# Other byte offsets for the stationary operands of a two-product MLP

## The chip, the core and the metric

The kernel runs on one NeuronCore of a Trainium2 chip. The metric is the device time of one execution in microseconds (us). The trace is one execution, taken by the hardware profiler. Its engines are TensorE (PE, with the loads of its stationary operand as PEld), VectorE (DVE), ScalarE (ACT), GpSimd (POOL) and SyncE (SP, which here issues DMAs).

## What is computed

A decoder layer on x of 2048 tokens by 1024 channels in float32. Its first half (input projection, mLSTM heads, causal convolutions, output projection) isn't touched. Its second half is the MLP:

```python
h2 = rms_norm(x, pre_mlp_norm_w[layer])
a = jax.nn.relu(jnp.einsum("bsd,df->bsf", h2, w_ff1[layer]))
m_out = jnp.einsum("bsf,fd->bsd", a * a, w_ff2[layer])
x = x + rms_norm(m_out, post_mlp_norm_w[layer])
```

with w_ff1 of 1024 x 4096 and w_ff2 of 4096 x 1024.

## The kernel before

It runs three phases one after the other: `phase_a` (input projection and convolutions), `phase_b` (mLSTM and output projection) and `phase_c` (the MLP). Each float32 product is made of three products of rounded parts: an operand is split by ScalarE into a high part (`_hi`) and by VectorE into the rest (`_lo`), and TensorE adds hi by hi, hi by lo and lo by hi in one PSUM bank. A matmul instruction is a load of the stationary operand (128 columns, 512 bytes of each partition) and a stream of the moving operand.

Both MLP products use a scheme with 7 sub-products in place of 8 (`OPS`, `OPS_2`). In the first product, `product(pe, op, g)` runs 12 matmuls of 512 columns (4 channel tiles, 3 pairs; L1861) for each of 7 sub-products and 32 groups: 2688 matmuls. Their stationary operand is a slice of 512 bytes of the weight tile `w1_hi[op]` (8 of the 12) or `w1_lo[op]` (4 of the 12), 14 tiles of 2 KB in all; the moving operand is a row of 2 KB of `x_hi` or `x_lo`. In the second product, `step(n)` runs 48 matmuls of 512 columns (L2079) for each of 56 steps, again 2688. Their stationary operand is a slice of 512 bytes of the middle activations `hid_hi` or `hid_lo`, which lie in a ring of 3 slots; the moving operand is a row of `w2_hi` or `w2_lo`. SyncE loads a slot of `hid_raw` two steps ahead (`load_hid`); ScalarE and VectorE split it in two halves each (`high_hid` L1952, `low_hid` L1957). VectorE reads the sums out of PSUM into the accumulators `acc`.

The order of every queue is written out by hand. Nothing chooses the addresses: in `phase_c`, `at(name, kb, ...)` places a tile at byte `4224 + 1024 * kb` of each partition. 4224 is 128 modulo 1024, so a tile at a whole `kb` has remainder 128, and one at a half `kb` has 640. Of the tiles that TensorE reads in phase C all have remainder 128, except buffer 0 of `x` and of `w2` (640, as moving operand). A slice of 512 bytes begins at 128 or 640.

In phases A and B the operands of the large matmuls (L404, L413, L423, L1332) begin at 128 or 640 too. One group doesn't: `("v", 0)` (L396) moves a row of 264 columns of the combined tile `vg_hi` or `vg_lo`. That tile begins at remainder 896, and each of its 8 rows (1056 bytes) lies 32 further modulo 1024: 896, 928, 960, 992, 0, 32, 64, 96. Its stationary operand (tokens) lies at 128 or 640.

Of the kernel before, what the change touches and what calls it, by code (L numbers as in the profile page):

```python
# [9 lines left out]
F32R = mybir.dt.float32r  # L10

P = 128
S = 2048
D = 1024
# [1631 lines left out]
OPS = ["P1", "P2", "P3", "P6", "P7", "P4", "P5"]  # L1646
# [60 lines left out]
def phase_c(nc, sem, psum, dram, late):  # L1707
# [6 lines left out]
    def at(name, kb, shape, dt=F32):  # L1714
        return nc.alloc_sbuf_tensor_at(name, [P, *shape], dt, offset=SB0 + int(1024 * kb))
# [2 lines left out]
    x_hi = [at(f"x_hi{i}", kb, (4, TB), F32R) for i, kb in enumerate(x_at)]  # L1718
    x_lo = [at(f"x_lo{i}", kb + 8, (4, TB), F32R) for i, kb in enumerate(x_at)]
    x_raw = [at(f"x_raw{i}", kb + 8, (4, TB)) for i, kb in enumerate(x_at)]  # L1720
    w1_hi = {op: at(f"w1_hi_{op}", 69 + 2 * i, (4, P), F32R) for i, op in enumerate(OPS)}
    w1_lo = {op: at(f"w1_lo_{op}", 83 + 2 * i, (4, P), F32R) for i, op in enumerate(OPS)}
    w1_raw = at("w1_raw", 187.5, (8, 4, P))
    c_1, c_x, c_7, c_21 = (at(n, 97 + 2 * i, (TB,)) for i, n in enumerate(("c_1", "c_x", "c_7", "c_21")))
    c_11 = at("c_11", 66, (TB,))
# [4 lines left out]
    w2_lo = [at(f"w2_lo{q}", kb + 8, (PIECE, TB), F32R) for q, kb in enumerate(w2_at)]  # L1730
    w2_raw = at("w2_raw", 170, (NFP, TB))
    grain = at("w2_grain", 161.5, (2, GRAIN, TB))
    hid_at = [121, 48, 105]
    hid_hi = [at(f"hid_hi{i}", kb, (NFP, P), F32R) for i, kb in enumerate(hid_at)]
    hid_lo = [at(f"hid_lo{i}", kb + 8, (NFP, P), F32R) for i, kb in enumerate(hid_at)]
    hid_raw = [at(f"hid_raw{i}", kb + 8, (NFP, P)) for i, kb in enumerate(hid_at)]
    acc = [at(f"acc{t}", 64 + 4 * t if t < 10 else 97.5 + 4 * t, (D,)) for t in range(S // P)]
    wpost = at("wpost_c", 170, (D,))
    junk = at("junk_c", 174, (D,))
    xn = at("xn_c", 178, (XN_RING, D))  # L1740
# [678 lines left out]
def build(nc, arrays, out):  # L2419
    scratch = {name: nc.dram_tensor("scratch_" + name, shape, dt).ap() for name, (shape, dt) in SCRATCH.items()}  # L2420
    dram = {**arrays, **scratch, "out": out.rearrange("a (n p) d -> (a n) p d", p=P)}
    with ExitStack() as ctx:  # L2422
# [3 lines left out]

        late = {}
        c = phase_c(nc, sem, psum, dram, late)
        b = phase_b(nc, sem, psum, dram, big, keep, c["prefetch"], late)
        a = phase_a(nc, sem, psum, dram, big, keep, b["tail"])  # L2430
# [42 lines left out]
```

## Time and profile before

| | us |
|---|---|
| median of 3 runs | 2109.27 |
| lowest and highest | 2109.08, 2110.45 |
| span of the profiled execution | 2109.4 |

The page of the profile gives the busy time of each engine, the clock that TensorE was granted, the chain of work that ended last, and the costliest groups of instructions. "x896 | 350.5, 391" means 896 instructions, 350.5 us in which at least one ran, 391 ns from start to end of one. Matmuls overlap in the pipeline, so what one costs is the distance from its start to the next one's start (here called the pitch), and not its 391 ns. The timeline gives the starts.

### The profile page before, as it was taken

To read this page: it belongs to the slowest core of one execution; us is meant where nothing else is said; L and a number is where in the kernel's file an instruction comes from. 1 tells how busy PE (TensorE), PEld (TensorE's weight loads), DVE (VectorE), ACT (ScalarE), POOL (GpSimd) and SP (SyncE) were. 2 spreads that over 40 slices of the span, in tenths; PEclk is the share of its full clock that TensorE was granted. 3 is DMA by queue.
4 is the path that set the end of the run, shared out by engine and by line. 5 is a ranking of instruction groups with operands and counts; after the bars stand their busy time and mean duration, and the time that the engine had idled before them with its cause. 6 is when DMAs were issued, how large, how long until landed. Compare 5 with 4: busy or idle time off the path is not lost. (4 is left out here: it accounts for less than half of the span.)

```text
span 2109.4 us, 26456 instructions
## 1 busy us (share of the span) xinstructions
PE 2065.3 (98%) x9843; PEld 1719.6 (82%) x9843; DVE 1441.5 (68%) x1979; ACT 913.2 (43%) x1545; POOL 414.6 (20%) x252
## 2 busy tenths in 40 slices
PE   7999999999999999899999999999999999999998
PEld 4897878878788888688888788888788888888887
DVE  5797999989567777876667866666663536534286
ACT  5633334343445444655445644554432313313163
POOL 0000000000001322333322322332262144400012
PEclk9999999999999999999999999999999999999999
DMA  5031212113656865854455655445766455443376
GB/s 201 11 101 51 70 40 77 54 30 107 195 165 205 264 225 167 269 175 136 153 164 179 235 165 157 138 145 172 254 227 249 163 206 187 167 167 137 140 250 219
DMA packets 253118, 338.53 MB, mean 160 GB/s; under 512 B 11584, under 2 KB 193600, under 8 KB 239168
## 3 DMA queue, kind: packets, MB, share of 16 engines
q1 hardware_dynamic: 220352, 315.80, 44.9%
q10 hardware_dynamic: 32384, 20.98, 3.1%
q8 instruction: 80, 1.31, 0.2%
q14 instruction: 46, 0.38, 0.1%
q0 software_dynamic: 256, 0.07, 0.0%
HBM read 225.58 MB, written 111.21 MB: 160 GB/s over the span
## 5 line engine op out<-in xcount | busy, mean ns | idle before, releaser
L1861 PE MATMUL psum<-x_hi,w_hi_P 128*128 128x512 f32 x896 | 350.5, 391 | 12.3 <-DVE x_lo L1805 6.2
L2079 PE MATMUL psum<-w_hi,hid_hi 128*128 128x512 f32 x896 | 349.3, 390 | 2.0 <-DVE hid_lo L1957 2.0
L1861 PE MATMUL psum<-x_lo,w_hi_P 128*128 128x512 f32 x896 | 349.6, 390 | 0.0
L1861 PE MATMUL psum<-x_hi,w_lo_P 128*128 128x512 f32 x896 | 349.5, 390 | 0.0
L2079 PE MATMUL psum<-w_lo,hid_hi 128*128 128x512 f32 x896 | 349.3, 390 | 0.0
L2079 PE MATMUL psum<-w_hi,hid_lo 128*128 128x512 f32 x896 | 349.1, 390 | 0.0
L1957 DVE TENSOR_TENSOR hid_lo<-hid_raw,hid_hi 128x1024 fp32r<-128x1024 f32 x112 | 176.7, 1615 | 207.4 <-ACT hid_hi L1952 207.3
L1774 POOL TENSOR_TENSOR w_raw<-w_raw 128x512 f32<-128x512 f32 x128 | 181.5, 1439 | 410.7 <-DVE w_lo_P L1787 388.5
L1952 ACT ACTIVATE hid_hi<-hid_raw 128x1024 fp32r<-128x1024 f32 x112 | 113.0, 1051 | 342.6 <-DMA hid_raw<-scratch_hid 342.6
L1787 DVE TENSOR_TENSOR w_lo_P<-w_raw,w_hi_P 128x512 fp32r<-128x512 f32 x224 | 184.6, 836 | 107.2 <-ACT w_hi_P L1783 104.2
L1783 ACT ACTIVATE w_hi_P<-w_raw 128x512 fp32r<-128x512 f32 x224 | 136.8, 627 | 255.7 <-PE psum L1861 249.3
L1861 PEld LDWEIGHTS psum<-x_hi,w_hi_P 128*128 128x128 f32 x896 | 168.9, 188 | 51.1 <-issue 14.4
L2079 PEld LDWEIGHTS psum<-w_hi,hid_hi 128*128 128x128 f32 x896 | 168.5, 188 | 37.4 <-issue 2.4
L1861 PEld LDWEIGHTS psum<-x_hi,w_lo_P 128*128 128x128 f32 x896 | 168.8, 188 | 35.0
L1861 PEld LDWEIGHTS psum<-x_lo,w_hi_P 128*128 128x128 f32 x896 | 168.8, 188 | 34.9
L2079 PEld LDWEIGHTS psum<-w_hi,hid_lo 128*128 128x128 f32 x896 | 168.6, 188 | 35.1
L2079 PEld LDWEIGHTS psum<-w_lo,hid_hi 128*128 128x128 f32 x896 | 168.5, 188 | 35.1
L1913 POOL TENSOR_TENSOR w_raw<-w_raw,w_grain 128x1024 f32<-128x1024 f32 x48 | 139.2, 2915 | 225.0 <-DMA w_grain<-in_w 225.0
L750 DVE SCALAR_TENSOR_TENSOR c_buf<-u_buf,par_a,c_buf 128x1024 f32<-128x1024 f32 x120 | 153.3, 1278 | 0.0
L750 DVE SCALAR_TENSOR_TENSOR c_odd<-u_buf,par_a,c_odd 128x1024 f32<-128x1024 f32 x112 | 143.1, 1277 | 4.2 <-ACT c_odd L556 4.2
L2204 DVE TENSOR_TENSOR c<-c,psum 128x512 f32<-128x512 f32 x96 | 65.5, 682 | 70.5 <-PE psum L1861 70.5
L423 PE MATMUL psum<-big_hi,w_hi 128*128 128x512 f32 x256 | 104.1, 407 | 4.0 <-DVE big_lo L704 3.7
(280 smaller groups left out, 3762.0 us busy)
## 6 DMA issues: line engine op xcount, KB each, us to landing
scratch_hid<-stage SPq DMA_DIRECT2D x224, 256.0 KB, 3.6
hid_raw<-scratch_hid SPq DMA_DIRECT2D x56, 1024.0 KB, 4.9
w_raw<-in_w SPq DMA_DIRECT2D x52, 1024.0 KB, 5.0
w_grain<-in_w SPq DMA_DIRECT2D x48, 512.0 KB, 5.0
x_raw<-scratch_h2s SPq DMA_DIRECT2D x14, 1024.0 KB, 8.5
w_raw<-in_w_in SPq DMA_DIRECT2D x22, 512.0 KB, 3.6
scratch_h2s<-h2s SPq DMA_DIRECT2D x8, 1280.0 KB, 9.2
scratch_qk<-qout ACTq DMA_DIRECT2D x16, 512.0 KB, 3.0
```

What stands on the lines that cost most here:

```text
L423: mm = nc.tensor.matmul(out, a, b, start=kt == 0 and i == 0, stop=kt == KT - 1 and i == 2)
L750: nc.vector.scalar_tensor_tensor(out=out, in0=u_buf[:, u % U_RING, k:k + HALF], scalar=par[:, CONV_W + g * CW + k:CONV_W + g * CW + k + 1] ...
L1774: nc.gpsimd.tensor_tensor(raw_1(op), raw_1(a), raw_1(b), ALU.subtract).then_inc(sem["w1_t"], 1)
L1783: nc.scalar.activation(w1_hi[op][:], raw_1(op), ACT.Copy).then_inc(sem["w1_hi"], 1)
L1787: nc.vector.tensor_tensor(w1_lo[op][:], raw_1(op), w1_hi[op][:].bitcast(F32), ALU.subtract).then_inc(sem["w1_lo"], 1)
L1861: mm = nc.tensor.matmul(psum[:, bank_1(op, g), :], l, r, start=kt == 0 and i == 0, stop=kt == 3 and i == 2)
L1913: nc.gpsimd.tensor_tensor(part, part, grain[:, n % 2], alu).then_inc(sem["w2_t"], 1)
L1952: nc.scalar.activation(hid_hi[n % HID_RING][:, half_fps(h)], hid_raw[n % HID_RING][:, half_fps(h)], ACT.Copy).then_inc(sem["hid_hi"], 1)
L1957: nc.vector.tensor_tensor(hid_lo[n % HID_RING][:, half_fps(h)], hid_raw[n % HID_RING][:, half_fps(h)], hid_hi[n % HID_RING][:, half_fps(h) ...
L2079: mm = nc.tensor.matmul(psum[:, bank, :], l, r, start=f == 0 and k == 0, stop=f == NFP - 1 and k == 2)
L2204: nc.vector.tensor_tensor(out[:], a[:], ps1(op, g), ALU.add).then_inc(sem["gather"], 1)
```

## The change

Only addresses change. The 14 weight tiles of the first product move down by 128 bytes or less, to the remainders 0, 0, 0, 32, 32, 32, 64 (`w1_hi`) and 64, 64, 96, 96, 96, 128, 128 (`w1_lo`), in the order P1, P2, P3, P6, P7, P4, P5. The 3 slots of the middle activations (high, low and raw alike) move up to the remainders 224, 192 and 160. The first ten accumulators move up by 96 bytes, out of the way of slot 1. The moving operands stay. On each of the five queues the built program has the same instructions in the same order with the same waits as before.

```diff
-    w1_hi = {op: at(f"w1_hi_{op}", 69 + 2 * i, (4, P), F32R) for i, op in enumerate(OPS)}
-    w1_lo = {op: at(f"w1_lo_{op}", 83 + 2 * i, (4, P), F32R) for i, op in enumerate(OPS)}
+    w1_hi = {op: at(f"w1_hi_{op}", 68.875 + 2 * i + i // 3 / 32, (4, P), F32R) for i, op in enumerate(OPS)}
+    w1_lo = {op: at(f"w1_lo_{op}", 82.875 + 2 * i + (7 + i) // 3 / 32, (4, P), F32R) for i, op in enumerate(OPS)}
...
-    hid_at = [121, 48, 105]
+    hid_at = [121 + 3 / 32, 48 + 1 / 16, 105 + 1 / 32]
...
-    acc = [at(f"acc{t}", 64 + 4 * t if t < 10 else 97.5 + 4 * t, (D,)) for t in range(S // P)]
+    acc = [at(f"acc{t}", 64 + 3 / 32 + 4 * t if t < 10 else 97.5 + 4 * t, (D,)) for t in range(S // P)]
```

## Rows read from the trace of the kernel before

**Rows 1.** The page: busy time of TensorE, granted clock, chain that ended last

```profile
PE 2065.3 (98%) x9843; PEld 1719.6 (82%) x9843; DVE 1441.5 (68%) x1979; ACT 913.2 (43%) x1545; POOL 414.6 (20%) x252
...
PEclk9999999999999999999999999999999999999999
...
PE 28%; DVE 1%; DMA 0%; SPq 0%; issue 0%; ACT 0%; DVEq 0%
```

**Rows 2.** Sums of stretches: us, busy (instructions) by engine, clock, DMA share, GB/s

```profile
core 0: us, PE busy (x) PEld busy (x) DVE busy (x) ACT busy (x) POOL busy (x), PEclk, DMA share, GB/s
...
900.00:1180.00 280.00, 280.00 (x1237) 231.93 (x1236) 191.67 (x271) 142.32 (x239) 82.96 (x60) 1.00 0.54 171
...
1520.00:2080.00 560.00, 560.00 (x2473) 463.68 (x2472) 287.65 (x289) 181.83 (x264) 149.34 (x52) 1.00 0.54 194
```

**Rows 3.** Timeline of TensorE, first product: start us, us, instruction; half clock until 895.98

```profile
892.14 0.63 PE L1861 MATMUL psum<-x_hi,w_lo_P 128*128 128x512 f32 x1
...
895.98 0.59 PE L1861 MATMUL psum<-x_hi,w_lo_P 128*128 128x512 f32 x1
896.41 0.40 PE L1861 MATMUL psum<-x_hi,w_hi_P 128*128 128x512 f32 x1
...
897.11 0.40 PE L1861 MATMUL psum<-x_hi,w_hi_P 128*128 128x512 f32 x1
897.35 0.39 PE L1861 MATMUL psum<-x_lo,w_hi_P 128*128 128x512 f32 x1
897.57 0.39 PE L1861 MATMUL psum<-x_hi,w_lo_P 128*128 128x512 f32 x1
...
898.73 0.39 PE L1861 MATMUL psum<-x_lo,w_hi_P 128*128 128x512 f32 x1
...
900.77 0.39 PE L1861 MATMUL psum<-x_lo,w_hi_P 128*128 128x512 f32 x1
```

**Rows 4.** Timeline of TensorE, output projection (L1332) after smaller matmuls

```profile
621.18 0.39 PE L1332 MATMUL psum<-big_lo,y_hi 128*128 128x512 f32 x1
...
622.79 0.39 PE L1332 MATMUL psum<-big_hi,y_lo 128*128 128x512 f32 x1
...
625.06 0.39 PE L1332 MATMUL psum<-big_hi,y_hi 128*128 128x512 f32 x1
```

**Rows 5.** Timeline of TensorE, 256-column matmuls (L413) after a small matmul

```profile
365.05 0.28 PE L413 MATMUL psum<-w_lo,big_hi 128*128 128x256 f32 x1
...
365.88 0.28 PE L413 MATMUL psum<-w_hi,big_lo 128*128 128x256 f32 x1
366.00 0.28 PE L413 MATMUL psum<-w_hi,big_hi 128*128 128x256 f32 x1
...
369.00 0.28 PE L413 MATMUL psum<-w_lo,big_hi 128*128 128x256 f32 x1
```

**Rows 6.** Timeline of TensorE, 264-column matmuls with changing remainders (L396)

```profile
129.80 0.28 PE L396 MATMUL psum<-w_lo,big_hi 128*128 128x264 f32 x1
...
134.39 0.28 PE L396 MATMUL psum<-w_hi,big_hi 128*128 128x264 f32 x1
```

**Rows 7.** Tile hid_raw: engine op xcount: duration ns min/median/max, first and last start

```profile
L1952 ACT ACTIVATE hid_hi<-hid_raw x112: 1040/1046/1064, 1476.9 to 2077.9; 128x1024 fp32r<-128x1024 f32 x112
L1957 DVE TENSOR_TENSOR hid_lo<-hid_raw,hid_hi x112: 1209/1225/3423, 1478.0 to 2079.7; 128x1024 fp32r<-128x1024 f32 x112
...
DMA to landing us min/median/max: 4.6/4.9/7.4
```

**Rows 8.** The page, costliest groups: the same VectorE operation on two tiles

```profile
L750 DVE SCALAR_TENSOR_TENSOR c_buf<-u_buf,par_a,c_buf 128x1024 f32<-128x1024 f32 x120 | 153.3, 1278 | 0.0
L750 DVE SCALAR_TENSOR_TENSOR c_odd<-u_buf,par_a,c_odd 128x1024 f32<-128x1024 f32 x112 | 143.1, 1277 | 4.2 <-ACT c_odd L556 4.2
```

## The prediction, made before the changed kernel was run

> **What bounds the kernel now.** I read the page first. TensorE is busy for 2065.3 of 2109.4 us, at 0.9 or more of the full clock in every slice, and the chain that ended last is made of it [rows 1]. Then the sums of two stretches, one inside each MLP product. There TensorE is busy for all of 280.00 and 560.00 us, while VectorE works 191.67 of 280 and 287.65 of 560 [rows 2]. So in phase C nothing but the pitch of the matmuls counts, and it can be read from the counts: 1237 records touch 280 us. A record is 0.39 us long, so about 1.7 of them only reach into the stretch: 280 / 1235.3 = 226.7 ns. The other stretch gives 560 / 2471.3 = 226.6 ns.
>
> [...]
>
> [...]
> [...]
> [...]
> - Behind an interruption they need some matmuls to settle. In the first product, 10 pitches from 896.41 to 898.73 have a mean of 232 ns (single ones lie apart: 897.11 to 897.35 is about 240, the next about 220), and then the 9 up to 900.77 have 226.7 [rows 3]. In the output projection, 7 pitches from 621.18 to 622.79 have 230 ns, and the next 10 have 227 [rows 4]. With 256 columns it is the other way: 7 pitches from 365.05 to 365.88 have 118.6 ns, and the settled ones 120.0 [rows 5].
>
> [...] The unsettled one is 3.3 to 5.3 ns longer at 512 columns, and 1.4 ns shorter at 256. All settled rows have both operands at the remainder 128 or 640.
>
> The one group that doesn't have them there is the 264-column one: 38 pitches from 129.80 to 134.39, 120.8 ns each [rows 6]. [...]
>
> **The change part by part.**
> - Weight tiles of the first product. The seven high tiles leave 128; of the low tiles five do. A group of 7 sub-products has 84 matmuls: 7 x 8 read a high tile and 5 x 4 a moved low tile, 76 in all; with 32 groups 2432. TensorE is the bound here, so each nanosecond on them is on the path.
> - Slots of the middle activations. All 2688 matmuls of the second product read a moved stationary operand. Together 5120.
> - What the new distance does to the pitch isn't in the trace for 512 columns. Bounds: above, the longest unsettled mean, 232 ns (+5.3 ns, 5120 x 5.3 = +27 us); one pitch of the same stretch is about 240 ns [rows 3], and if a fixed distance held the pair at 236, halfway between that and the mean, it would be +9.3 ns, +48 us. Below, the 264-column row, -2.5 ns (5120 x 2.5 = -13 us). Between them: the settled pitch stays, 0. I take the mean of the two unsettled 512-column rows, 231 ns, +4.3 ns, since these are the rows with the same length of stream, and the 264-column row is nearest to them in kind (unsettled) but has the stream of the 256-column rows, where unsettled is the cheap side. 5120 x 4.3 = **+22.0 us**.
> - Splits and loads of the middle activations at new remainders. ScalarE's 1046 and VectorE's 1225 ns, and 4.9 us to landing [rows 7]. For VectorE the trace has one operation on two tiles at the remainders 416 and 896 (c_buf, c_odd), 1278 and 1277 ns [rows 8], so 0. The DMA's price at another remainder isn't shown, nor ScalarE's. Both have cover: a slot is loaded two steps ahead, 96 matmuls or 21.8 us, and load and splits take 4.9 + 2 x 1.05 + 2 x 1.23 = 9.5 us in a row. The load could double to 9.8 us and the sum, 14.4, would still fit. Only the first steps (the start of the second product) and the last stores lack that cover; a tenth of 4.9 us there is 0.5 us. I count 0, and keep 1 us for the range.
> - Accumulators 96 bytes further: VectorE adds into them beside TensorE's work, and its idle third of the stretch [rows 2] hides 10 ns more on each. 0.
> - Nothing is late that wasn't: no instruction moves, no wait is added. If matmuls get longer, VectorE, ScalarE and the DMAs have more cover; if they get 2.5 ns shorter, 12 of them save 0.03 us of 2.72, and VectorE at 68% doesn't become the bound.
>
> The sum is made on the profiled execution, 2109.4, which lies 0.1 over the median of 2109.27. 2109.3 + 22.0 = **2131.3 us**.
>
> **The rivals.**
> 1. [...] If all 13.3 ns went, as they do at half clock [rows 3], it would be 5120 x 13.3 = 68 us, 2041.2; no settled or unsettled mean in the rows comes near that, so I give all results far below 2092 together 4 in 100.
>    [...]
> [...]
> 3. *The change doesn't do what it says*, so that addresses are as before. They are given as fixed bytes and nothing rounds them to more than 4; 1 in 100, inside rival 2.
> 4. *Worse than unsettled.* A fixed distance that meets the load's reads again and again: 236 ns, 2109.3 + 48 = 2157. One or two of the eight remainders may do this while others do nothing; the mean would fall back near my sum.
>
> **How the numbers follow.** Slower by an unsettled pitch (+10 to +35 us) 42 in 100; worse (over +35) 8; a little slower (+4.2 to +10, some of the remainders settle) 4; nothing 19; faster near -13 us 20, faster by less 3, faster by far more 4. A run of this kernel tells some 0.2% from nothing, 4.2 us. So slower 54, same 19, faster 27. The range reaches from the 264-column case, with 1 us for the DMAs and 0.7 ns of reading error in its mean, to the fourth rival: 2092 to 2156. The likeliest case alone has 2119 to 2144.
>
> **What would show it.** In the profile after, the count of matmuls in a stretch in which TensorE is always busy: at 231 ns it is 1214 in 280 us in place of 1237, at 224.2 it is 1251. The first product's stretch grows by 2432 x 4.3 = 10.5 us, the second's by 11.6. If only some tiles matter, the pitches within one group of 84 matmuls differ by sub-product, as their tiles have different remainders, and so do the steps of the second product in a cycle of three. Phases A and B keep their times. Were the difference in phase A or B, or in waits of TensorE on hid_lo, my reading would be wrong; so it would be if every pitch stayed at 226.7.

## The result: slower by 1.3%, on the matmuls whose stationary operand was moved

| | before | changed |
|---|---|---|
| median of 4 runs, us | 2109.86 | 2137.11 |
| lowest and highest, us | 2109.08, 2111.05 | 2135.86, 2140.79 |
| span of the profiled execution, us | 2109.4 | 2139.0 |

The ratio is 1.0132, with a 95% interval of 1.0117 to 1.0146. The profiled execution is the slowest of the four (2140.79); its own difference is 29.6 us, the median's 27.3.

From the page of the changed kernel (busy time, clock, two groups; for the groups the fields are those of [rows 8]):

```profile
PE 2097.3 (98%) x9843; PEld 1721.5 (80%) x9843; DVE 1440.9 (67%) x1979; ACT 911.9 (43%) x1545; POOL 416.5 (19%) x252
...
PEclk9999999999999999999999999999999999999999
...
L1861 PE MATMUL psum<-x_hi,w_hi_P 128*128 128x512 f32 x896 | 355.6, 397 | 10.9 <-DVE x_lo L1805 5.8
L2079 PE MATMUL psum<-w_hi,hid_hi 128*128 128x512 f32 x896 | 354.8, 396 | 1.1 <-DVE hid_lo L1957 1.1
```

TensorE is busy 32 us longer [rows 1], VectorE, ScalarE and GpSimd as long as before, and the clock is the same. The sums of stretches of the changed kernel, with the columns of [rows 2]:

```profile
900.00:1180.00 280.00, 280.00 (x1209) 226.76 (x1208) 186.43 (x264) 137.09 (x232) 83.45 (x60) 1.00 0.53 162
1550.00:2080.00 530.00, 530.00 (x2270) 426.73 (x2269) 257.53 (x265) 162.03 (x226) 128.94 (x45) 1.00 0.50 180
```

A record is again taken to reach 1.7 pitches over the edges. In the first product the pitch is 280 / 1207.3 = 231.9 ns, in the second 530 / 2268.3 = 233.7 ns, where both were 226.7 [rows 2]. 2688 x 5.2 + 2688 x 7.0 = 32.8 us.

The starts of the first matmul of each product tell where the rest is. The first product lasts 640.6 us where it was 628.5, 12.1 more and not 14.0; pitches over 242 ns, its interruptions, are 1.6 us shorter in sum. The second lasts 629.1 us where it was 612.9, 16.2 more and not 18.8. There the difference is the first three steps: before they took 3.8 us more than three steps at the settled pitch, now 1.3. The remaining 1.3 of the 29.6 us passed before the first product begins. That can't be laid to the change: among the profiled executions with the weight tiles where they were, it begins anywhere from 858.7 to 862.7 us.

At half clock nothing changed. The granted clock is 0.50 ahead of the second weight group, and there 9 pitches of the changed kernel take 895.87 - 892.03 = 3.84 us, 426.7 ns each, as in [rows 3]:

```profile
892.00:895.80 3.80, 3.80 (x10) 2.97 (x9) 3.80 (x5) 0.72 (x2) 3.72 (x3) 0.50 0.83 276
```

```profile
892.03 0.63 PE L1861 MATMUL psum<-x_lo,w_hi_P 128*128 128x512 f32 x1
...
895.87 0.63 PE L1861 MATMUL psum<-x_lo,w_hi_P 128*128 128x512 f32 x1
```

And in the second product it isn't noise but a fixed length for each slot. The first matmuls of four steps in a row in the second product (timeline, 48 pitches between two rows):

```profile
1695.53 0.40 PE L2079 MATMUL psum<-w_hi,hid_hi 128*128 128x512 f32 x1
...
1706.73 0.40 PE L2079 MATMUL psum<-w_hi,hid_hi 128*128 128x512 f32 x1
...
1717.97 0.39 PE L2079 MATMUL psum<-w_hi,hid_hi 128*128 128x512 f32 x1
...
1729.16 0.40 PE L2079 MATMUL psum<-w_hi,hid_hi 128*128 128x512 f32 x1
```

The step in slot 2 (32 bytes off) takes 11.20 us, that in slot 0 (96 bytes) 11.24, that in slot 1 (64 bytes) 11.19; before it was 48 x 226.7 ns = 10.88. By the starts inside such steps the pitches repeat: 235, 232 in slot 2; 231, 236 in slot 1; a cycle of seven from 230 to 238 in slot 0, means 233.4, 233.2 and 234.3. After the first three steps each visit of a slot repeats its mean within 0.1 ns.

### The profile page after: what moved, and what is told of

Read it like the earlier page. It is cut to its first block and busy times, and to the rows that moved or that the text cites. A ratio compares the mean times of both kernels' runs of the same rounds, so it can differ in the third digit from the quotient of the medians.

```text
span 2139.0 us, 26456 instructions
## 1 busy us (share of the span) xinstructions
PE 2097.3 (98%) x9843; PEld 1721.5 (80%) x9843; DVE 1440.9 (67%) x1979; ACT 911.9 (43%) x1545; POOL 416.5 (19%) x252
## 5 line engine op out<-in xcount | busy, mean ns | idle before, releaser
L1861 PE MATMUL psum<-x_hi,w_hi_P 128*128 128x512 f32 x896 | 355.6, 397 | 10.9 <-DVE x_lo L1805 5.8
L2079 PE MATMUL psum<-w_hi,hid_hi 128*128 128x512 f32 x896 | 354.8, 396 | 1.1 <-DVE hid_lo L1957 1.1
L2079 PE MATMUL psum<-w_lo,hid_hi 128*128 128x512 f32 x896 | 354.7, 396 | 0.0
L2079 PE MATMUL psum<-w_hi,hid_lo 128*128 128x512 f32 x896 | 354.4, 396 | 0.0
L1861 PE MATMUL psum<-x_hi,w_lo_P 128*128 128x512 f32 x896 | 353.9, 395 | 0.0
```

Source lines behind the costliest of these rows:

```text
L1861: mm = nc.tensor.matmul(psum[:, bank_1(op, g), :], l, r, start=kt == 0 and i == 0, stop=kt == 3 and i == 2)
L2079: mm = nc.tensor.matmul(psum[:, bank, :], l, r, start=f == 0 and k == 0, stop=f == NFP - 1 and k == 2)
```

## The experiments

Below, "distance" is the remainder of the stationary operand less that of the moving one, modulo 512 bytes (a slice of 512 bytes steps through 128 and 640, so 512 is 0). e1 to e4 ran on one chip, e5 to e11 on a second and e12 on a third, each beside the kernel before (medians from 2108.4 to 2109.8 us).

### One part of the change alone

```diff
 e1_slots_only (against before)
-    hid_at = [121, 48, 105]
+    hid_at = [121 + 3 / 32, 48 + 1 / 16, 105 + 1 / 32]
-    acc = [at(f"acc{t}", 64 + 4 * t if t < 10 else 97.5 + 4 * t, (D,)) for t in range(S // P)]
+    acc = [at(f"acc{t}", 64 + 3 / 32 + 4 * t if t < 10 else 97.5 + 4 * t, (D,)) for t in range(S // P)]
 e2_weights_only (against before): the two lines of w1_hi and w1_lo of the change
```

> Only the 3 slots of the middle activations (and the first ten accumulators) lie as in the changed kernel; the 14 weight tiles lie as before. If the pitch of each matmul whose stationary operand was moved is what costs, the second product keeps the 233.7 ns that its stretch 1550:2080 has in the changed kernel, the first product goes back to 226.7 ns, and the time is 2688 x 7.0 ns = 18.8 us over before, 2128. If instead the splits or loads of the middle activations at odd remainders were what costs, TensorE would show waits on hid_hi or hid_lo in the second product and its pitch would be near 226.7.

> Only the 14 weight tiles lie as in the changed kernel; the slots and accumulators as before. If the cost lies in the moved matmuls alone, the first product has 231.9 ns and the second 226.7, and the time is 2688 x 5.2 ns = 14 us over before, less some 3 us of waits of the first product that longer matmuls cover: 2120 to 2124. If the two parts act on each other (one product's layout costs in the other), the sum of both parts alone misses the 27 us of the whole change by more than 4 us.

Slots alone: 2124.79 us, ratio 1.0071 (1.0056 to 1.0086). Weights alone: 2120.06 us, ratio 1.0051 (1.0034 to 1.0067). Before, beside them: 2109.48. The two stretches of slots alone, then of weights alone:

```profile
900.00:1180.00 280.00, 280.00 (x1237) 231.96 (x1236) 191.79 (x272) 142.25 (x238) 82.42 (x59) 1.00 0.55 171
1550.00:2080.00 530.00, 530.00 (x2270) 427.03 (x2269) 254.70 (x269) 168.01 (x243) 118.55 (x42) 1.00 0.50 182
```

```profile
900.00:1180.00 280.00, 280.00 (x1209) 226.80 (x1208) 187.41 (x265) 137.63 (x232) 80.42 (x58) 1.00 0.53 164
1550.00:2080.00 530.00, 530.00 (x2340) 438.87 (x2339) 268.60 (x276) 171.20 (x247) 130.11 (x46) 1.00 0.53 190
```

Each part slows its own product to the very count of the changed kernel (2270, 1209) and leaves the other at that of before (1237; 2340 is 530 / 2338.3 = 226.7 ns). They take 15.3 and 10.6 us more than before, 25.9 together, beside 27.3 for both: they add up. 15.3 is under the 18.8 that I expected of the slots, although the pitch is as expected; the profiled execution, 2124.7 against 2109.4, also gives 15.3. The missing 3 us lie in the first three steps of the second product: they take 1.0 us more than three settled steps here and 3.8 before, and the whole product takes 628.7 - 612.9 = 15.9 us longer. This part isn't owed to the slots alone: in e2_weights_only, where they lie as before, it is 2.2 us. The accumulators' new place isn't told apart from the slots' here; the next run has the same accumulators and clears them.

### The distance, not the remainder 128

```diff
 e3_both_moved (against before)
-    w2_at = [203.5, 0, 32, 16]
+    w2_at = [kb + 3 / 32 for kb in (203.5, 0, 32, 16)]
-    hid_at = [121, 48, 105]
+    hid_at = [kb + 3 / 32 for kb in (121, 48, 105)]
-            act.wait_ge(sem["st1"], st1(["P2", "P3", "P6", "P7"][f // PIECE], NGRP - 1))
+            act.wait_ge(sem["st1"], st1(["P2", "P7", "P4", "P7"][f // PIECE], NGRP - 1))
 and acc, t < 10: 64 + 3 / 32; eps_c at 219.59375, ss_c at 219.625
```

> In the second product both operands lie 96 bytes further than before: the 3 slots and the 4 buffers of w2 (hi and lo), so stationary and moving operand have the same remainder again, 224 or 736. The four pieces of the first w2 wait for later products of the last group (P2, P7, P4, P7 in place of P2, P3, P6, P7), since they now overlap two x buffers; that may cost up to 10 us once, ahead of the second product. The weight tiles lie as before. If the distance of the two remainders decides, the stretch 1550:2080 goes back to 226.7 ns. If the remainder 128 itself is what is cheap, every matmul there has an operand off it and stays at 233 ns or more: 18 us more in the second product.

2108.73 us, ratio 0.9993 (0.9983 to 1.0002), the same as before. Its second product:

```profile
1550.00:2080.00 530.00, 530.00 (x2340) 438.85 (x2339) 273.12 (x282) 175.14 (x259) 123.67 (x44) 1.00 0.53 192
```

The slots lie 96 bytes off 128 here, as slot 0 does in the changed kernel. With the moving operand 96 bytes off as well, the count is that of before, 2340. So it is the distance between the two operands that costs, and neither the remainder, nor the splits, nor the loads at an odd address, nor the accumulators, which lie here as in the changed kernel. This is shown for the one distance that both operands were moved by, 96 bytes.

### The sweep of distances

```diff
 e4_sweep_a (against before): hid_at = 121 + 256 B, 48 + 128 B, 105 + 32 B; w1_hi and w1_lo: all 128 B lower
 e5_sweep_b: hid_at = 121 + 480 B, 48 + 448 B, 105 + 416 B; w1 tiles interleaved (hi at 69 + 4 * i, lo at 71 + 4 * i), lower by
             128, 96, 96, 64, 64, 32, 0 B in the order of OPS
 e6_sweep_c: hid_at = 121 + 512 B, 48 + 320 B, 105 + 384 B
 e9_fine: slots of hid at 48, 40 and 16 B; all w1 tiles 16 B lower (views into tiles that are a little larger)
 e12_eight: slots of hid at 136, 72 and 24 B; all w1 tiles 120 B lower
 in each the first ten accumulators move out of the way of slot 1
```

> A sweep of distances, read from the pitch. Slots 0, 1, 2 of the middle activations lie 256, 128 and 32 bytes behind the moving operand's remainder; all 14 weight tiles lie 128 bytes ahead of it, high and low alike. If only the distance 0 (modulo 512) settles at 226.7, all four have 230 to 236 ns. If the period is 128 bytes, the slots 0 and 1 and the whole first product are back at 226.7 and only slot 2 has 233.4. If it is 256 bytes, slot 0 alone is back. If slot 2 shows the 233.4 that slot 2 has in the changed kernel at the same distance, the pitch belongs to the distance and not to the slot.

> The other side of the sweep. Slots 0, 1, 2 of the middle activations lie 480, 448 and 416 bytes behind the moving operand's remainder, which is -32, -64 and -96 modulo 512 (and modulo 256). The weight tiles are interleaved so that the high and the low tile of one sub-product have the same distance: -128 (P1), -96 (P2, P3), -64 (P6, P7), -32 (P4), 0 (P5). If the sign plays no part, the slots repeat the 233.3, 233.2 and 234.3 ns of +32, +64 and +96. If load and stream chase each other through SBUF, the sign matters and some of the three are under 230 or over 236 ns. None is under 226.7 if that is the floor.

> The period. Slots 0, 1, 2 lie 512, 320 and 384 bytes behind the moving operand's remainder, the weight tiles as before. With a period of 256 bytes (as the 227.2 ns at 256 suggest) slot 0 has 226.7, slot 1 the 233.2 of 64, slot 2 the 232.5 of 128. With a period of 512 slot 0 has 226.7 and the two others differ from these values by over 1 ns.

> Distances between the steps of 32: slots 0, 1, 2 at 48, 40 and 16 bytes, all weight tiles at -16, with 512 columns. If only multiples of 256 settle at 226.7 and this is the floor, all four have 230 to 236 ns. If the grain is 32 bytes, the distance 16 behaves as 0 (226.7) and 40 and 48 as 32 (233.4). A pitch under 226.7 would show that the aligned layout is not the best one.

> With distances of 16, -16 and 40 the pitch settled at 226.7, with 32, 48, 64, 96, 128 it didn't. Here slots 0, 1, 2 lie at 136, 72 and 24 bytes, all weight tiles at -120, all of them 8 bytes off a multiple of 16. If an offset of 8 within 16 bytes is what let 40 settle, all four are at 226.7 and the time is that of before, 2109. If 40 settled because small distances do (and 48 and 32 are exceptions), 24 is at 226.7 and 72, 136 and -120 at 231 to 235, and the time is near 2130.

One execution each: 2136.53, 2132.95, 2120.78, 2118.9 and 2140.4 us. What is wanted from them is the pitch, from steps as above. Two of the timelines; of e4_sweep_a (slot 2, then 0, then 1):

```profile
1696.20 0.40 PE L2079 MATMUL psum<-w_hi,hid_hi 128*128 128x512 f32 x1
...
1707.40 0.39 PE L2079 MATMUL psum<-w_hi,hid_hi 128*128 128x512 f32 x1
...
1718.31 0.41 PE L2079 MATMUL psum<-w_hi,hid_hi 128*128 128x512 f32 x1
...
1729.46 0.40 PE L2079 MATMUL psum<-w_hi,hid_hi 128*128 128x512 f32 x1
```

and of e9_fine (slot 0, then 1, then 2; L2088 is the line of the second product there):

```profile
1693.34 0.40 PE L2088 MATMUL psum<-w_hi,hid_hi 128*128 128x512 f32 x1
...
1704.54 0.39 PE L2088 MATMUL psum<-w_hi,hid_hi 128*128 128x512 f32 x1
...
1715.42 0.39 PE L2088 MATMUL psum<-w_hi,hid_hi 128*128 128x512 f32 x1
...
1726.30 0.40 PE L2088 MATMUL psum<-w_hi,hid_hi 128*128 128x512 f32 x1
```

In the first, 32 bytes take 11.20 us, 256 bytes 10.91, 128 bytes 11.15. In the second, 48 bytes take 11.20, 40 bytes 10.88, 16 bytes 10.88. All that was measured with 512 columns, as the mean pitch by the starts to the nanosecond, over whole steps behind the first few (second product) or over the groups from 900 to 1180 us (first product, high and low tile at one distance):

| distance, bytes | ns | from |
|---|---|---|
| 0, 512 | 226.7, 226.8 | before, e6 |
| 16, -16 | 226.8, 226.7 | e9 slot 2, e9 weights |
| 24 | 230.1 | e12 slot 2 |
| 32, -32 | 233.4 and 233.3, 233.2 | after and e4 slot 2, e5 slot 0 |
| 40 | 226.7 | e9 slot 1 |
| 48 | 233.2 | e9 slot 0 |
| 64, -64 | 233.2; 229.1 or 233.5 | after slot 1, e5 slot 1 |
| 72 | 233.3 | e12 slot 1 |
| 96, -96 | 234.3, 233.3 | after slot 0, e5 slot 2 |
| -120, 136 | 233.3, 233.3 | e12 weights, e12 slot 0 |
| 128, -128 | 232.4, 232.4 | e4 slot 1, e4 weights |
| 256 | 227.2 | e4 slot 0 |
| 320, 384 | 233.3, 232.5 | e6 slots 1, 2 |

What follows. As far as it was measured, the period is 256 bytes: 320 and 384 (233.3, 232.5 ns) repeat 64 and 128 (233.2, 232.4), in mean and in the cycle of pitches (236, 231 for both 64 and 320). And 256 is as good as 0: of its 48 pitches the first eight, behind a step at another distance, have a mean of 229.4 ns, and the rest 226.8. Nothing measured with 512 columns is under 226.7. The sign changes the mean by at most 1.0 ns (96 and -96), but for the one state of -64 that is told of below. Near 0 it isn't smooth, though: 16, -16 and 40 are within 0.1 ns of 226.7, 24 costs 3.4 ns, 32 and 48 cost 6.5 to 6.7. My guess for e12, that 8 bytes off a multiple of 16 are harmless, failed at all four places; that small distances are harmless fails at 24 and 32. I can't give a rule for this.

At -64 the same slot has two states. Its steps take 11.0 us or 11.2, by turns from the third visit on. Two steps of e5_sweep_b, the second and the tenth visit of slot 1:

```profile
1544.67 0.39 PE L2080 MATMUL psum<-w_hi,hid_hi 128*128 128x512 f32 x1
...
1555.66 0.39 PE L2080 MATMUL psum<-w_hi,hid_hi 128*128 128x512 f32 x1
...
1812.43 0.40 PE L2080 MATMUL psum<-w_hi,hid_hi 128*128 128x512 f32 x1
...
1823.63 0.40 PE L2080 MATMUL psum<-w_hi,hid_hi 128*128 128x512 f32 x1
```

The first two rows are one step (229.0 ns a pitch), the last two the other (233.5 ns). Step n writes the PSUM bank `(n + 1) % 8`, so in this slot odd and even banks alternate as the two pitches do. But the two steps shown (n = 4 and 28) both write bank 5, and both read the same addresses of the slot and of w2. So the address doesn't set the pitch alone; what went before picks one of several repeating cycles. That it is the timing at the entry is my reading, which no run shows; none varied it alone.

### Which of the neighbours counts

```diff
 e8_lo_apart (against before)
-    hid_at = [121, 48, 105]
+    hid_at = [121 + 1 / 4, 48 + 1 / 8, 105]
+    lo_at = [129 + 3 / 8, 56 + 1 / 4, 113 + 3 / 32]
 hid_lo and hid_raw at lo_at; acc, t < 10: 64 + 1 / 4
```

> Which of the two neighbours counts. In slot 0 the high part lies at 256 (as good as 0) and the low part at 384 (as 128); in slot 1 the high part at 128 and the low part at 256; in slot 2 the high part at 0 and the low part at 96. Weight tiles as before. Of each three matmuls (high with w2_hi, high with w2_lo, low with w2_hi) the load of the low part runs beside the second stream. If what counts is the stream beside which a load runs, in slots 0 and 2 the second pitch of three is the one off 226.7, and in slot 1 the first and the third. If what counts is the matmul's own pair, it is the third in slots 0 and 2 and the first two in slot 1. If the state is carried from one matmul to the next, all three are off, and the means lie between 226.7 and the 232.5 or 234.3 of a slot that is apart as a whole.

2121.03 us in one execution. In slot 0 (high part at 256, low at 384) the timeline reads:

```profile
1697.32 0.39 PE L2080 MATMUL psum<-w_hi,hid_hi 128*128 128x512 f32 x1
1697.55 0.40 PE L2080 MATMUL psum<-w_lo,hid_hi 128*128 128x512 f32 x1
1697.78 0.40 PE L2080 MATMUL psum<-w_hi,hid_lo 128*128 128x512 f32 x1
1698.01 0.39 PE L2080 MATMUL psum<-w_hi,hid_hi 128*128 128x512 f32 x1
...
1698.71 0.39 PE L2080 MATMUL psum<-w_hi,hid_hi 128*128 128x512 f32 x1
1698.93 0.40 PE L2080 MATMUL psum<-w_lo,hid_hi 128*128 128x512 f32 x1
1699.17 0.40 PE L2080 MATMUL psum<-w_hi,hid_lo 128*128 128x512 f32 x1
1699.40 0.39 PE L2080 MATMUL psum<-w_hi,hid_hi 128*128 128x512 f32 x1
```

By the starts to the nanosecond the three pitches repeat as 226.7, 232.5, 234.3. The second is the stream beside which the low part is loaded (in the trace the load starts 2 to 3 ns after it and lasts 188 ns), and it is off, as the first theory says. The third is off too, although the load beside it is of a high part at a good distance: that is the second theory's, or the carried state. The first recovers, once some 12 matmuls of the step have passed. In slot 1 (128, 256) all are off, 232, 233, 235; in slot 2 (0, 96) all vary, mean 232.4. So neither theory holds alone. Both together would give slots 0 and 1; in slot 2 the first pitch of three is off too (231 to 236), and neither theory gives that; that something is carried over from the matmuls before is my reading. A single bad load in three costs 5.0 ns a matmul on the mean of the step (231.7), nearly as much as the 5.7 of three (128 bytes for all, e4 slot 1).

### Streams of 256 columns

```diff
 e7_halves, e10_halves_b (against before)
-            for f in range(NFP):
+            for c, f in ((c, f) for c in range(2) for f in range(NFP)):
...
+                cols = slice(TB // 2 * c, TB // 2 * (c + 1))
+                hi, lo = w2_part(w2_hi, f)[:, cols], w2_part(w2_lo, f)[:, cols]
 e7: slots as in the change (96, 64, 32 B); e10: 192, 128, 0 B
```

> The slots lie as in the changed kernel (96, 64, 32 bytes behind), but each matmul of the second product is two of 256 columns, first all of the left halves of a step, then all of the right ones; twice the loads, 5376 matmuls. Weight tiles as before. If a distance costs because a sequence never settles, and unsettled is cheap at 256 columns as after an interruption (118.6 ns against 120.0), the pitch is under 120.0. If a distance makes each load cost the stream more, whatever its length, it is 120.0 + 6.7 = 126.7 or more. The second product then takes 5376 x 118.6 = 638 us or 5376 x 126.7 = 681 us, in place of 628.

> The second product in halves of 256 columns again, with the slots 0, 1, 2 at 192 (which is -64), 128 and 0. At distance 0 I expect the 120.0 ns of the 256-column rows of before, not the 113.3 of distance 64. If the length of the stream and the distance act together, -64 and 128 differ from each other and from 120. If the halves of slot 1 were short by something other than the distance, slot 1 is at 113.3 again here.

2146.12 and 2144.64 us in one execution each. Steps of 96 pitches, of e7_halves (slots 0, 1, 2), then of e10_halves_b (slots 0, 1, 2):

```profile
1698.86 0.28 PE L2080 MATMUL psum<-w_hi,hid_hi 128*128 128x256 f32 x1
...
1710.38 0.28 PE L2080 MATMUL psum<-w_hi,hid_hi 128*128 128x256 f32 x1
...
1721.27 0.28 PE L2080 MATMUL psum<-w_hi,hid_hi 128*128 128x256 f32 x1
...
1732.63 0.28 PE L2080 MATMUL psum<-w_hi,hid_hi 128*128 128x256 f32 x1
```

```profile
1696.68 0.28 PE L2080 MATMUL psum<-w_hi,hid_hi 128*128 128x256 f32 x1
...
1707.56 0.28 PE L2080 MATMUL psum<-w_hi,hid_hi 128*128 128x256 f32 x1
...
1718.95 0.28 PE L2080 MATMUL psum<-w_hi,hid_hi 128*128 128x256 f32 x1
...
1730.46 0.28 PE L2080 MATMUL psum<-w_hi,hid_hi 128*128 128x256 f32 x1
```

| distance | 0 | 32 | 64 | 96 | 128 | 192 |
|---|---|---|---|---|---|---|
| 256 columns, ns | 119.9 | 118.3 | 113.4 | 120.0 | 118.6 | 113.4 |
| 512 columns, ns | 226.7 | 233.4 | 233.2 | 234.3 | 232.4 | 229.1 or 233.5 (as -64) |

At 96 bytes the step isn't always the same: of 17 steps without a stop 11 have 120.0 ns, two 118.7 and four 117.3. At 256 columns none of these distances costs more than 0.1 ns over distance 0, and 64 and 192 save 6.6 ns. Distance 64, which costs 6.5 ns at 512 columns, is among the cheapest at 256. So at 64 the two lengths have opposite signs.

These two kernels also have 256-column matmuls at the granted clock 0.50. In e10_halves_b at distance 0, then in e7_halves at distance 64:

```profile
1865.20:1868.00 2.80, 2.80 (x15) 2.80 (x14) 2.80 (x3) 0.00 (x0) 0.00 (x0) 0.50 0.86 295
```

```profile
1865.23 0.41 PE L2080 MATMUL psum<-w_hi,hid_hi 128*128 128x256 f32 x1
...
1867.79 0.41 PE L2080 MATMUL psum<-w_hi,hid_hi 128*128 128x256 f32 x1
```

```profile
1680.45:1683.10 2.65, 2.65 (x15) 2.65 (x14) 2.27 (x3) 0.00 (x0) 0.00 (x0) 0.50 0.84 278
```

```profile
1680.45 0.41 PE L2080 MATMUL psum<-w_hi,hid_hi 128*128 128x256 f32 x1
...
1683.01 0.41 PE L2080 MATMUL psum<-w_hi,hid_hi 128*128 128x256 f32 x1
```

Both are 12 pitches in 2.56 us, 213.3 ns each, half of the 426.7 of 512 columns [rows 3]. So at clock 0.50 the pitch goes with the columns and leaves nothing over. At the full clock it doesn't: 512 columns have 226.7 ns at distance 0 and 256 have 120.0, so 106.7 ns go with 256 columns, and 120.0 - 106.7 = 13.3 are left. That is an estimate of what lies on top of the stream; 226.7 - 426.7 / 2 gives the same. By it 264 columns at distance 0 would have 120.0 + 106.7 x 8 / 256 = 123.3 ns, and the group of [rows 6] has 120.8. The sign at 256 columns may be why it is shorter than that; no run moved that group.

That both kernels take some 36 us longer than before says nothing against this. Two matmuls of 256 columns cost more than one of 512 (239.8 ns for 226.7 at distance 0): over the whole product some 630 us, where 2688 at 226.7 ns take 609.3. And six steps of each kernel, the first ones on new weights, take 19 us in all over the pitches of the table; in the second product of e7_halves TensorE's listed waits are for w_lo (L1934), 6.9 us, and part of two of the six steps runs at half clock. Those steps aren't in the table.

### The other way round, in the input projection

```diff
 e11_v_pair (against before; the second pair of v tiles, 384 matmuls of 256 columns)
+V_SHIFT = 48
+V_TILES = [TILES.index(("v", 2)), TILES.index(("v", 3))]
-            return a[:, KT * GATE_COLS:].rearrange("p (r k d) -> p r k d", r=W_RING, k=KT)
+            return a[:, KT * GATE_COLS + by:w_cols + by].rearrange("p (r k d) -> p r k d", r=W_RING, k=KT)
-            return ring_tiles(a)[:, RING[t]]
+            return ring_tiles(a, V_SHIFT if t in V_TILES else 0)[:, RING[t]]
 pads of the same sum keep all other operands' remainders; one weight load waits for one more slot
```

> The finding turned round, in the input projection: MLP as before, but the second pair of v tiles lies 192 bytes further in its ring slots (384 of the 672 matmuls of 256 columns at L413 of before), so that their stationary operand is 64 bytes behind the moving one's remainder, modulo 256. Pads make room; no other operand of a matmul changes its remainder, and one weight load waits for one more slot. If the 113.3 ns that 256 columns had at the distance 64 in slot 1 of the halves belong to the distance, these 384 matmuls take 113.3 ns in place of 120.0: 2.6 us less, 2107. If they belong to that place in the program alone, 120 ns and 2109.5, or 116 to 122 ns as in the other two slots.

2107.78 us over 12 runs, ratio 0.9994 (0.9986 to 1.0003): no difference that can be told. Two rows of its timeline, 33 pitches apart:

```profile
366.10 0.28 PE L417 MATMUL psum<-w_lo,big_hi 128*128 128x256 f32 x1
...
369.98 0.28 PE L417 MATMUL psum<-w_lo,big_hi 128*128 128x256 f32 x1
```

3.88 / 33 = 117.6 ns, where it was 120.0 [rows 5]: less, but not the 113.3 of the same distance in the halves. In all 384 matmuls this is 0.9 us. Here the moving row comes in two pieces of 128 columns that lie 4096 bytes apart, in the halves in one; whether that is why is open. No version clearly beats the kernel before.

## Why the prediction was right, and where it was not

- **What bounds the kernel.** Right. The pitch of the 5376 matmuls was all that the change acted on; TensorE's stretches stay fully busy (280.00 of 280, 530.00 of 530 us), and the time follows their counts (1209 for 1237, 2270 for 2340).
- **The 13.3 ns that would all go.** No run shows this term of the 68 us by itself; it is the author's estimate. What the runs show is 426.7 ns at clock 0.50 where the full clock has 226.7 [rows 3], and a pitch that at clock 0.50 goes with the columns and at the full clock leaves 13.3 ns over. By the same estimate, with nothing changed but one operand's address relative to the other's, they became 20 ns at 512 columns (233.4 ns at distance 32), and half of them went at 256 columns (113.4 ns for 119.9). At clock 0.50 nothing is over in the changed kernel either (426.7 ns). How much it is depends on the length of the stream: at distance 64 it is 19.9 ns at 512 columns (233.2 ns) and 6.7 at 256 (113.4). That the load and the stream get in each other's way is the author's guess; what collides wasn't shown.
- **The size, 4.3 ns on each of 5120.** Too small. The pitch is 5.2 ns longer over the first product and 7.0 over the second; 6.4 ns for each moved matmul. The step that was too small is the choice of the mean of the two rows that follow an interruption (230 and 232 ns). The upper one would have been near in the first product (231.9 ns) and still too low in the second (233.7). These rows show a sequence on its way to the settled 226.7 ns, so they hold good pitches too. 2131.3 was forecast, 2137.1 measured. That these lie only 5.8 us apart is in part luck: by the pitch alone the forecast was 10.8 us short (22.0 for 32.8), and 4 to 5 us of it were offset by shorter interruptions, which the sum had put at nothing and which differ from execution to execution.
- **An unsettled pitch.** Wrong in kind. A fixed distance does settle, mostly within a dozen matmuls, in a short cycle of pitches (2 in one slot of the changed kernel, 7 in another); the cycle's mean is what costs, 233.2 to 234.3 ns in its three slots. That is nearest to the fourth rival, a fixed distance that costs again and again, which had 8 in 100; its 236 ns were too high, the worst slot has 234.3. (By its own sum it ends at 2157, 1 us outside the stated range.) So the forecast had the place, the sign and about the size, and held the wrong picture of the state to be the likeliest.
- **The 2.5 ns of the 264-column row, 20 in 100 for faster near -13 us.** No run shows this term of the lower bound and of the range, nor that the row is unsettled: none has 264 columns at a fixed distance. The row has 120.8 ns [rows 6], and 123.3 for distance 0 is an estimate from the pitches of 256 and 512 columns. Rightly put behind slower: the runs with halves show that a distance can be cheaper than 0 at 256 columns and dearer at 512 (113.4 for 119.9 ns and 233.2 for 226.7, at 64), so a row of the shorter stream was no guide to the sign.
- **Nothing, 19 in 100.** Settled pitches of 226.7 to 226.8 ns form at 16, -16 and 40 bytes, and 227.2 in the mean of the steps at 256, but not at every fixed distance; of these distances the change has none. That a pitch settles doesn't make the cost 0: in the changed kernel it settles at 233.2 to 234.3 ns.
- **Splits, loads, accumulators at 0.** Right: ScalarE 1047 and VectorE 1225 ns, 4.9 us to landing in the changed kernel, as in [rows 7], and e3_both_moved at 0.9993.

From the tile page of hid_raw in the changed kernel:

```profile
L1952 ACT ACTIVATE hid_hi<-hid_raw x112: 1035/1047/1063, 1489.9 to 2106.3; 128x1024 fp32r<-128x1024 f32 x112
L1957 DVE TENSOR_TENSOR hid_lo<-hid_raw,hid_hi x112: 1210/1225/3433, 1491.0 to 2108.2; 128x1024 fp32r<-128x1024 f32 x112
...
DMA to landing us min/median/max: 4.6/4.9/7.9
```

## What to carry to other kernels

Where TensorE is the bound and streams 512 float32 columns per load, give the stationary and the moving operand the same remainder modulo 256 bytes (226.7 to 226.8 ns here); against most distances from 32 to 128 bytes (232.4 to 234.3 ns) it was worth 2.5 to 3.4% of the pitch, and cost only padding. Judge it from the count of matmuls in a fully busy stretch (1209 for 1237), and not from a record's own length (397 for 391 ns). Don't carry the rule to 256-column streams untested: there the same remainder (119.9 ns) was at most 0.1 ns better than another measured distance, and 6.6 ns slower than 64 or 192 bytes in the MLP, 2.4 ns slower than 64 in the input projection.

## What the runs showed that I had not expected

- Several settled pitches lie 6.7 ns apart: 113.3 and 120.0 ns at 256 columns, 226.7 and 233.3 at 512, which is 6.7, 13.3 and 20.0 ns over half of what the same columns take at clock 0.50 (213.3 and 426.7 ns). At 256 columns 13.3 is not the least of it; at 512 nothing measured was below it.
- The same instructions on the same addresses can settle at different pitches: 229.1 or 233.5 ns at -64 with 512 columns, 117.3, 118.7 or 120.0 at 96 with 256.
- 16 bytes and 40 bytes are harmless (226.7 to 226.8 ns), 24, 32 and 48 are not (230.1, 233.4 and 233.2). This is open.
